# Joining the value projections of the two strided dilated groups into products of 512 columns

## The reference

```python
# u = rmsnorm(x), one combined projection with 4992 output columns:
cols = jnp.split(u @ w_in_l, splits, axis=-1)
aq, af, ai, ag, bq, bk, bv = cols[:7]             # recurrent heads (a), differential attention (b)
dil = tuple(tuple(c.reshape(n, t, H_C, DH_C) for c in cols[7 + 3 * g: 10 + 3 * g])
            for g in range(len(DILATED_PAIRS)))   # q, k, v of 256 columns each, for three dilated groups
DILATED_PAIRS = ((128, 1), (512, 4), (2048, 16))
```

## Time and profile before

| | |
|---|---|
| median of 3 runs | 1049.95 us (1045.94 to 1050.38) |
| the profiled execution's own time | 1055.73 us |
| its span, first to last instruction | 1054.0 us |
| TensorE matmul busy | 948.5 us, 90% of the span |
| VectorE, ScalarE, GpSimd busy | 376.9, 238.2, 81.5 us |
| granted TensorE clock, mean of the span | 0.948 of full speed |
| differential attention with woven projections, blocks 6 to 23 | 297.7 to 440.4 us of the span |

### The profile page before, as it was taken

How to read it: one execution, slowest core, us unless ns; L and a number is a source line. 1 busy time by engine, 2 the same in 40 slices (tenths; PEclk the granted TensorE clock), 3 DMA queues, 4 the chain that set the end, 5 groups by cost and what they waited for, 6 DMA issues and landing times.

```text
span 1054.0 us, 15610 instructions
## 1 busy us (share of the span) xinstructions
PE 948.5 (90%) x6377; PEld 492.1 (47%) x6377; DVE 376.9 (36%) x791; ACT 238.2 (23%) x600; POOL 81.5 (8%) x96
## 2 busy tenths in 40 slices
PE   3996999999999998986969983899999999998886
PEld 2453556655456785663444543333333333333442
DVE  4305644564226755355542226111111111111445
ACT  3115212221232332443221110000000000003335
POOL 1000000000024531000000000100000000002100
PEclk9999999999999998969788995899999999999998
DMA  6463433035357651247323419298999999994101
GB/s 209 167 233 150 91 140 140 1 140 175 140 177 244 218 171 43 98 138 208 124 79 130 187 51 390 79 344 332 378 373 381 398 395 392 401 379 132 41 21 62
DMA packets 69138, 209.55 MB, mean 199 GB/s; under 512 B 19113, under 2 KB 51332, under 8 KB 62540
## 3 DMA queue, kind: packets, MB, share of 16 engines
q1 hardware_dynamic: 54384, 185.53, 47.8%
q0 software_dynamic: 3936, 14.22, 4.1%
q10 hardware_dynamic: 10748, 8.80, 2.6%
HBM read 189.09 MB, written 38.26 MB: 216 GB/s over the span
## 4 chain that ended last, share of the span: by engine, by line
PE 80%; DVE 8%; DMA 4%; ACT 4%; issue 2%; SPq 2%; ACTq 0%; POOL 0%; DVEq 0%; POOLq 0%
PE ps L1959 16%; PE ps L2369 11%; PE ps L1964 9%; PE ps L2262 6%; PE ps L2406 5%; PE ps L2485 5%; PE ps L2365 5%; DMA EXPERT<-in_moe_w_up 2%; PE ps L1994 2%; PE ps L2331 2%; PE ps L2040 2%; PE ps L2354 1%; PE ps L1968 1%; PE ps L2402 1%; PE ps L2121 1%
## 5 line engine op out<-in xcount | busy, mean ns | idle before, releaser
L1959 PE MATMUL ps<-xT,EXPERT 128*128 128x512 f32 x384 | 178.3, 610 | 1.2 <-DVE xS L1299 1.2
L1964 PE MATMUL ps<-EXPERT,xT 128*128 128x384 f32 (+1 forms) x384 | 121.6, 459 | 1.6 <-ACT EXPERT L959 1.6
L1959 PEld LDWEIGHTS ps<-xT,EXPERT 128*128 128x128 f32 x384 | 71.1, 195 | 77.3 <-issue 73.9
L1964 PEld LDWEIGHTS ps<-EXPERT,xT 128*128 128x128 f32 x384 | 78.7, 239 | 24.5 <-issue 3.6
L1871 DVE TENSOR_TENSOR dF<-dF,ps 64x512 f32<-64x512 f32 (+1 forms) x24 | 14.4, 601 | 185.3 <-ACT dF L1191 185.3
L2485 PE MATMUL ps<-EXPERT 128*128 128x512 f32 x128 | 56.0, 596 | 5.3 <-DVE EXPERT L1920 5.3
L2262 PE MATMUL ps<-EXPERT,xT 128*128 128x512 f32 x128 | 59.5, 617 | 0.8 <-ACT xT L1127 0.8
L2369 PE MATMUL ps<-EXPERT,samp 128*32 128x512 f32 x384 | 57.8, 594 | 0.0
L2369 PE MATMUL ps<-EXPERT,wk 128*32 128x512 f32 x448 | 53.2, 619 | 2.1 <-DMA EXPERT<-in_moe_w_up 1.1
L1195 ACT ACTIVATE dF<-ps 128x256 f32<-128x256 f32 (+1 forms) x24 | 8.3, 348 | 163.7 <-PE ps L2389 163.7
L1023 ACT ACTIVATE wk<-ps,small 128x128 f32<-128x128 f32 (+3 forms) x48 | 24.9, 522 | 85.5 <-DVE small L1460 85.5
(11 more groups left out here) (457 smaller groups left out, 1353.2 us busy)
## 6 DMA issues: line engine op xcount, KB each, us to landing
EXPERT<-in_moe_w_gate SPq DMA_DIRECT2D x12, 2048.0 KB, 19.4
EXPERT<-in_moe_w_up SPq DMA_DIRECT2D x12, 2048.0 KB, 14.8
EXPERT<-in_moe_w_down SPq DMA_DIRECT2D x12, 2048.0 KB, 17.2
EXPERT<-in_w_in SPq DMA_DIRECT2D x13, 1536.0 KB, 6.6
out_win_sample<-in_cache_win SPq DMA_DIRECT2D x16, 1022.0 KB
aF<-in_cache_k_diff SPq DMA_DIRECT2D x32, 192.0 KB, 2.5
aF<-in_cache_v_diff SPq DMA_DIRECT2D x32, 192.0 KB, 2.5
Yd<-wk ACTq DMA_DIRECT2D x34, 128.0 KB, 8.5
```

Source lines behind the costliest of these rows:

```text
L1959: last = t.matmul(ps[:, u % 2, :], W_[:, c, c0:c0 + w], xT[:, c, 0:SEQ], start=(c == 0), stop=(c == DC - 1))
L1964: last = t.matmul(ps[:, u % 2, 0:w], rows_, W_[:, c, c0:c0 + w], start=(c == 0), stop=(c == DC - 1))
```

## The change

Slabs 10 and 12 lie in the two buffers at the same time. Their TM units are joined: under one stationary load of 128 strided tokens, 256 value columns of slab 10 and 256 of slab 12 stream past in one product of 512 columns, four units in place of eight, and ScalarE copies 128x512 to both groups' values at once. Slab 10 keeps SM and FM; slab 12 has the four joined units first, then SM, then FM. The last unit that reads slab 10's buffer is now the last joined one, so the load of slab 3 is asked for behind it. There are 57 units in place of 61.

```diff
+BOTH = (10, 12)
@@ projection_units
+            elif s == BOTH[0]:
+                units += [("FM", s, 0, P, (7 + g, 3))]
+            elif s == BOTH[1]:
+                units += [("TM", s, P, 4 * P, (None, i)) for i in range(NT)]
+                units += [("FM", s, 0, P, (7 + g, 3))]
             else:
                 units += [("FM", s, 0, P, (7 + g, 3))]
                 units += [("TM", s, P, 2 * P, (7 + g, i)) for i in range(NT)]
@@ unit_marks
+    last[BOTH[0]] = max(u for u in range(len(units)) if units[u][0] == "TM" and units[u][1] == BOTH[1])
@@ schedule, project_one
-        at = ORDER.index(units[u][1])
-        if u == last[units[u][1]] and c1 == DC and at + 2 < NSLAB:
+        at = [ORDER.index(sl) for sl in range(NSLAB) if last[sl] == u]
+        if at and c1 == DC and at[0] + 2 < NSLAB:
+            at = at[0]
             steps.append(("slab", at + 2))
@@ ScalarE
+                elif kind == "TM" and at[0] is None:
+                    dst, src = cvT[:, 1:3, at[1]], src.rearrange("p (g n) -> p g n", g=2)
@@ TensorE
+                    elif kind == "TM" and at[0] is None:
+                        both = EXPERT[:, 0:2 * DC * SLAB].rearrange("p (k c n) -> p k c n", k=2, c=DC)
+                        last = t.matmul(ps[:, u % 2, :].rearrange("p (g n) -> p g n", g=2), cols(xT[:, c, 0:SEQ])[:, at[1]],
+                                        both[:, :, c, P:3 * P], start=(c == 0), stop=(c == DC - 1))
```

## The result

The changed kernel takes 1058.6 us in the median of 18 runs (1055.07 to 1065.68), the kernel before 1049.95 in 18 runs beside it (1043.56 to 1054.6): ratio 1.0093, 95% interval 1.0071 to 1.0115. The forecast was 1047.4, its range ended at 1053.5. The profiled execution took 1065.58 us, 7 over its median, so single stretches of it are compared with care; a second profile of each kernel stands with the experiments.

A forecast was written before the change was run, and what follows sets the result against it. TensorE was taken to bound the kernel, holding 80% of the chain. Terms -4.6 - 4.0 - 3.1 + 1.4 + 1.1 + 5.6 + 1.0 = -2.6 us gave 1047.4 us against the median 1049.95; range 1042.5 to 1053.5.

The forecast's parts named there:

- The first, since the products of 512 columns have 109 ns to spare over the 327: Joined products: the strided weight load stays wholly hidden, -4.6 us; the other bound was -2.6.
- The key loads queued behind it on SyncE have buffers that VectorE frees later anyway: SyncE's queue at slab 3's load: moving that load's issue delays no key load and costs nothing.
- It is just covered: -4.0 us: Stall at dec_new: 10.3 us of TensorE work cover the 10.2 us path to block 16's weighing, saving 4.0 us.
- 3.1 us at half clock: Behind the dec_new stall: without the stall the half-clock stretch goes too, -3.1 us.
- rival 4: At d_t(16): the dec_new stall stays, cover exceeding the path by 0.1 us only; 1053.5, up to 1054.5 us; 7%.
- d_t(10): Start of slab 10: TensorE arrives earlier and waits for block 10's weighing, +1.4 us.
- Slab 12's load: First joined product: slab 12 is needed 21 us sooner and lands late, +1.1 us, bounds 0 to +2.8.
- The tail, +5.6: From d_s(21) to c_s(0): projections run out and TensorE waits for VectorE and ScalarE; 15.4 us, +5.6.
- +1.0: Clock behind the tail: c_s(0) may run at half clock, +1.0 us.
- rival 3: The clock falls in the tail itself, doubling its TensorE work (+4.2) and work behind (+3.9); 1054.5 us; 11%.
- forecast -3.6: Sum of the terms without the clock behind the tail: c_s(0) some 3.6 us sooner than 440.4.

The follow-up runs named there:

- e8: The changed kernel with joined products taking 128 neighbouring tokens instead of strided ones, so some values are wrong; one run, 1058.32 us.
- e4: The changed kernel with the key load issued ahead of slab 3's load in SyncE's queue; 1062.72 us, ratio 1.0077 to the kernel before.
- e3: The changed kernel with dec_new one block later, behind d_s(17); 1057.12 us, ratio 1.0065 to the kernel before.
- e5: The changed kernel with slab 12's load issued ahead of the key load before it; 1056.67 us, ratio 1.0064 to the kernel before.
- e16: The changed kernel in its own order, its joined products cut in two of 256 columns; 1061.67 us, ratio 1.0105 to the kernel before.
- e6: The changed kernel with the projection share per step lowered to 0.9 from step 51; 1053.49 us, ratio 1.0033 to the kernel before.
- e12: The changed kernel with dec_new behind d_s(17) and share 0.9 from step 51, slab 12's load unmoved; 1053.14 us, ratio 1.0006.
- e11: The kernel before, products apart, with only dec_new moved, behind d_s(20); 1045.69 us, ratio 0.9936 to the kernel before.
- e7: The changed kernel with the edits of e5, e3 and e6 together; 1051.26 us, ratio 0.999 to the kernel before.
- e1: The changed kernel with three units of slab 3 computed a second time to fill the tail; 1070.31 us, ratio 1.0154 to the kernel before.
- e13: The changed kernel with slab 12's load first, dec_new from step 51, share 1.6, then 1.3 from step 40; 1044.41 us, ratio 0.9932.
- e15: The kernel of e13 with its joined products cut in two of 256 columns, same order; 1043.78 us, ratio 0.9932 to the kernel before.

## Why the prediction was wrong

By its own steps, on the way to c_s(0), in the first profile:

- *"The first, since the products of 512 columns have 109 ns to spare over the 327"*: the term was mis-sized. The products take 33.0 us before and 29.3 now, so -3.7 in place of -4.6. The load is hidden beside products of 512 columns, as said; left out was the first load of each of the ten series of products, 0.12 us each (e8), and for the kernel before that a series of four records takes more than half of what one of eight takes.
- *"The key loads queued behind it on SyncE have buffers that VectorE frees later anyway"*: failed, by 2.7 us. VectorE had freed the buffer by 376.1, SyncE stood before slab 3's load until 378.33, and the keys went out behind it. But another 11.6 us of the product's delay are VectorE's own later dec_q, of which the prediction has no word. GpSimd's product came 11 us behind the keys, exactly where the weighing had been put. That keys on time would have saved the term is not shown. In e4 the product began 4.9 us behind the start of dec_new and not 6.8, and it cost VectorE 4.2 us in place of 3.0.
- *"It is just covered: -4.0 us"*: this is the step that failed. The path from the sample unit to the end of the weighing was counted as 10.2 us, with nothing of GpSimd beside it; it took 13.2, 3.65 us of them in an operation of 0.62, against 10.5 us of cover. 2.78 us of 4.03 stayed, and 1.7 of 3.1 us at half clock: -2.7 in place of -7.1. This was rival 4, put at 7%, for a reason that it did not name, though the earlier trace rows showed it at block 10.
- *d_t(10)*: right in the first profile, 1.27 for 1.4, and no wait in the second, where GpSimd's product missed that weighing. *Slab 12's load*: right in the first profile, 1.44 for 1.1, landing 9.4 us after its issue; but 0 to 3.67 us over the ten profiles that leave its place, with half clock behind those from 2.34 on. A single value was too sure.
- *The tail, +5.6, and "+1.0" for the clock behind it*: the waits came as said, rising (0.66, 1.60, 2.13), but the clock fell inside the tail. From the end of d_s(21), 426.4, to c_s(0) are 17.7 us, not 15.4: +7.9. The step that failed is the end of it: up to d_t(23) it took 13.3 us, as reckoned, and then d_t(23) and two d_pv took 4.35 us at half clock, where 2.0 had been reckoned. e3, e5 and e16 pay the same 4.35, though there the clock fell only at the third gap. That is rival 3's mechanism, put at 11%; but its +4.2 doubled all of the tail's work, where only what stands behind the last wait counts.

Sum: -3.7 - 2.7 + 1.3 + 1.4 + 7.9 = +4.2, read off as +3.7; forecast -3.6.

Behind c_s(0) the prediction took +1.0. By the ratio it is 5.4 of 9.8 us, and every kernel with joined products shows a loss there, 2.1 us at the least; it is clear of its interval in the change, e3, e5 and e6, barely or not in the others. Where two profiles were set side by side it is TensorE's clock (e12 against e11). What follows the first output product takes 495.8 to 500.4 us in all profiles, so a few us of scatter lie there too. What sets it is not settled: not the tail alone (e6, e7 and e12 lose 2.3 to 4.1 us without its gaps), not the tokens of the stationary operand (e8's one profile has 110.4 us), not the hour of arrival (e1 arrives 10 us later, e13 14 us sooner, and both lose 2 us). Width or order of the products stays open after e15 and e16. The stretch lengths alone would not show it: 108 to 123 us in twelve profiles with joined products, 111 to 114 in the six without (e15 and e16 among them). The Trainium skill, "TensorE: Matmul & The Clock Gate", section "What's actually happening", has the number of products done at half clock at the start of a kernel vary between runs of one kernel. Here it is a stretch in the middle that varies, 119.7 and 114.4 us for the same program, at 0.73 and 0.74 of full clock.

What the change was worth: in the order it came with, +8.65 us. With its waits ordered away, 3.9 us at c_s(0) against the kernel before in its own better order, all of it in the products (29.2 us against 33.0), and in the whole time nothing that 12 runs each can tell.

## What to carry to other kernels

Before you book a stall as covered, look in the trace at what GpSimd runs while VectorE has the operations of the path, and follow where the new list moves GpSimd's work to. Products saved in a woven schedule are filler taken from some later step: spread what is left before you measure, and try the same reordering on the kernel before, for it may be the gain (here 5.8 us for one line). When work is equal and the time isn't, compare equal stretches by the granted clock, in more than one profile.

## What was not expected of the hardware

- A weight load of 128 strided float32 columns has a record of 308 ns, of neighbouring ones 190 ns. Behind products of 512 columns the difference costs nothing; it costs its 0.12 us once, at the first product of a series that follows shorter work (e8).
- The length of a wait did not decide the clock. 1.60 us in the tail was followed by half clock in the change, not in e3, e5 and e16; 2.78 and 2.79 us at d_t(16) were in the change's first profile and in e6, not in its second and in e1. Waits of 1.44 us and less never were in this stage.
- In e12 TensorE was busy for 19.98 of 20.00 us at a granted clock of 0.57.
- The load of slab 12, 1.5 MB, landed 8.6 to 10.0 us after its issue in ten profiles of changed kernels with a set of key loads just ahead of it, and 7.5 to 9.1 us when issued before them (e5, e7, e13, e15). Slab 3's took 6.5 to 6.8 us, and 10.4 behind a set of key loads (e4).
